# Three modulation weight units behind the experts, per-block waits at the layers' seams

## The chip, the cores and the metric

The kernel runs on one core of one Trainium2 chip. The metric is the device time of one execution in microseconds (us), less is better. Five engines run their own instruction streams and meet only at semaphores: PE (TensorE, matrix products into PSUM), DVE (VectorE), ACT (ScalarE), POOL (GpSimd) and SP (SyncE, which here issues nearly all DMAs, strictly in program order).

## The reference, cut to what matters

Three networks run one after the other on 256 tokens of width 1024, in fp32:

```
x = first_block(x, c, ...)    # Fourier + recurrent mixer, then a mixture of 16 experts
    h = modulate(rms_norm(x), sh2, sc2)
    gate, idx = top_k(softmax(h @ w_router), 32)          # each expert takes 32 of 256 tokens
    hid = silu(xs @ w_g[e]) * (xs @ w_u[e])               # 1024 -> 2816, e = 0..15
    x = x + gt2 * segment_sum((hid @ w_d[e]) * gate)      # 2816 -> 1024
x = second_block(x, c_2, ...) # attention and spatial gating, then relu^2 MLP
    x = x + gate1 * (merged @ w_out);  x = x + gate2 * (square(relu(h @ w_ff1)) @ w_ff2)
x = third_block(x, c_3, ...)  # two layers
    for l in (0, 1):
        shift, scale, gate = split(silu(c_3) @ w_ada_3[l] + b_ada_3[l], 3)     # 1024 x 3072
        proj = (rms_norm(x) * (1 + scale) + shift) @ w_in_3[l]
        x = x + gate * rms_norm(mix(proj) @ w_out_3[l])
```

The modulation of the third block's layer 0 (`w_ada_3[0]`) depends on `c_3` alone, so it may be computed at any time before that layer.

## The kernel before, in words

**Weights.** All weights stream once from HBM. A *unit* is one ring slot of 1.5 MB: 8 x 128 rows by 384 columns of a dense layer, or one 128-row piece of a modulation matrix (`w_ada`). `Plan` deals the units to four ring slots in the order of `CYCLE`; a unit's load is issued by SP once the unit before it in the slot is used (`unit_used`, counted by PE). During the expert stage the ring, the arena and `w_hi_raw` are twelve slots. An expert has 14 units (`EXPERT`); the first seven of expert 0 (`FIRST_CYCLE`) are loaded ahead, those of two slots in halves (`load_half`), and every later unit waits for PE to use the unit before it in its slot.

**Modulations.** `ada[p]` are eight units, each multiplied by `ada_unit` (16 matmuls into PSUM banks 6 and 7), copied out by ACT (`rows_out`), turned by PE (`turn`) and added to the bias by DVE (`mod_in`). `ada[4]`, the one for the third block's layer 0, is loaded and multiplied in the stage between the first block's mixer and expert 0.

**Dense layers.** A layer is cut into blocks of 128 output features, three to a unit. Each fp32 weight block is split in two parts: ACT copies the high part (`high_parts`, L1281, into one of four `w_hi` buffers), DVE subtracts for the low part (`low_parts`, L1684, counted as `w_split`). A block is then 24 matmuls: high x high, low x high, high x low, for eight chunks k of the input. The first three blocks of a layer run k-outer (`k_outer`, L769): for every chunk k the matmuls of all three blocks, so that they can start before the input is complete. The others run block by block (L818). Before its first matmul `k_outer` waits for the splits of all three blocks.

**Norms.** In the second and third block the RMS factor is applied behind the matmul ("raised"): ACT and DVE make the parts of a scaled X (`raise_x` L1309, `raise_low` L1813), squares are summed on DVE (L1793, L1805, L2101), PE adds over partitions (`column_sums` L849, L853), ACT takes the root, DVE the reciprocal (L1846), and only then can DVE empty the PSUM banks (`scale_rows` L1854). PE can run up to six blocks before that. `row_roots` lets DVE split the weight block `s0 + 4` between the sums' result and the reciprocal, where `s0` is the layer's first block; `s0 + 5` follows behind three `scale_rows`.

The seams are: experts to in2, proj2 to out2, out2 to ff1, ff2 to in3[0], in3[0] to out3[0], out3[0] to in3[1], in3[1] to out3[1].

## Time and profile before

| | us |
|---|---|
| median of 3 runs | 2250.39 (2247.58 to 2255.58) |
| the profiled execution, its own time | 2241.95 |
| its span in the trace | 2239.6 |
| PE busy | 1698.4 (76%) |
| DVE busy | 797.6 (36%) |
| ACT busy | 525.1 (23%) |
| mean granted TensorE clock, share of full speed | 0.857 |

The profiled execution took 2.35 us more than its span and 8.4 us less than the median of the runs. Busy shares are means over stages with different limits: the expert stage fills the middle of the span, and the dense layers stand on either side of it.

### The profile page before, as it was taken

What the parts mean: (1) busy time and instruction counts of PE and PEld (TensorE: products, weight loads), DVE (VectorE), ACT (ScalarE), POOL (GpSimd) and SP (SyncE); (2) the same over time, 40 slices, a digit from 0 to 9 for tenths busy, and PEclk for the clock granted to TensorE, in tenths of its full rate; (3) what the DMA queues carried; (4) which work ended last, traced back from release to release, by engine and by line L of the source; (5) the groups of instructions that cost most, each with busy time, mean ns of one, the idle gap of its engine ahead of it and who ended that gap; (6) DMA issues with size and microseconds to landing.
All of it is one profiled execution on the core that took longest, in us unless ns stands there. A gap on an engine that the chain in (4) does not pass through costs nothing.

```text
span 2239.6 us, 33790 instructions
## 1 busy us (share of the span) xinstructions
PE 1698.4 (76%) x14864; PEld 1168.7 (52%) x14864; DVE 797.6 (36%) x1237; ACT 525.1 (23%) x857; POOL 52.6 (2%) x85
## 2 busy tenths in 40 slices
PE   5999986656766666665665755665899999999897
PEld 4896843313322322322331322232798999998896
DVE  5766630000000000000000000010775788788777
ACT  2420220000000000000000000000574564365664
POOL 0014000000000000000000000000000000000000
PEclk8999997877777777777777787877999999999999
DMA  9877899999999999999999999999743559853541
GB/s 357 291 269 298 350 414 428 427 428 429 432 430 428 431 429 429 430 430 429 428 431 428 428 431 430 428 429 429 233 156 133 170 180 348 280 171 125 168 133 66
DMA packets 138723, 760.60 MB, mean 340 GB/s; under 512 B 7911, under 2 KB 96743, under 8 KB 106888
## 3 DMA queue, kind: packets, MB, share of 16 engines
q1 hardware_dynamic: 134968, 754.06, 83.7%
q10 hardware_dynamic: 3664, 5.24, 0.7%
q8 instruction: 68, 1.11, 0.2%
q14 instruction: 23, 0.19, 0.0%
HBM read 756.13 MB, written 3.14 MB: 339 GB/s over the span
## 4 chain that ended last, share of the span: by engine, by line
DMA 48%; PE 43%; DVE 6%; ACT 1%; issue 1%; SPq 1%; DVEq 0%; ACTq 0%
DMA ring<-in_w_exp_down 27%; PE ps L818 19%; DMA ring<-in_w_exp_up 18%; PE ps L1103 4%; PE ps L1233 4%; PE ps L1096 4%; DMA w_hi_raw<-in_w_exp_up 3%; PE ps L769 3%; DVE ring_lo L1684 1%; PE ps L692 1%; PE ps L1215 1%; PE ps L964 1%; PE ps L812 1%; PE ps L1148 1%; PE ps L874 0%
## 5 line engine op out<-in xcount | busy, mean ns | idle before, releaser
L1103 PE MATMUL ps<-arena,const 128*32 128x352 f32 x2816 | 340.6, 644 | 255.7 <-DMA arena<-in_w_exp_up 136.2
L1103 PEld LDWEIGHTS ps<-arena,const 128*32 128x32 f32 x2816 | 107.3, 143 | 476.0 <-DMA arena<-in_w_exp_up 170.9
L1684 DVE TENSOR_TENSOR ring_lo<-ring,w_hi 128x1024 fp32r<-128x1024 f32 x220 | 267.4, 1219 | 43.7 <-ACT w_hi L1281 42.7
L818 PE MATMUL ps<-u_hi,w_hi 128*128 128x258 f32 x960 | 275.5, 287 | 1.3 <-DVE ring_lo L1684 1.1
L2065 DVE TENSOR_TENSOR tail<-tail,ps 128x704 f32<-128x704 f32 x15 | 13.3, 888 | 734.4 <-PE ps L1103 734.4
L818 PE MATMUL ps<-u_hi,ring_lo 128*128 128x258 f32 x960 | 271.2, 282 | 0.0
L818 PE MATMUL ps<-u_lo,w_hi 128*128 128x258 f32 x960 | 271.0, 282 | 0.0
L1281 ACT ACTIVATE w_hi<-ring 128x1024 fp32r<-128x1024 f32 x220 | 230.2, 1050 | 69.0 <-PE ps L1233 30.5
L818 PEld LDWEIGHTS ps<-u_hi,w_hi 128*128 128x128 f32 x960 | 181.6, 189 | 7.3 <-issue 5.2
L1103 PE MATMUL ps<-ring,const 128*32 128x352 f32 x1024 | 126.0, 656 | 77.8 <-DMA ring<-in_w_exp_up 40.6
L818 PEld LDWEIGHTS ps<-u_lo,w_hi 128*128 128x128 f32 x960 | 181.6, 189 | 0.0
L818 PEld LDWEIGHTS ps<-u_hi,ring_lo 128*128 128x128 f32 x960 | 181.2, 189 | 0.0
L1096 PE MATMUL ps<-ring,const 128*32 128x256 f32 x1536 | 128.8, 503 | 58.1 <-DMA ring<-in_w_exp_down 58.1
L2069 DVE TENSOR_TENSOR arena<-arena,ps 128x2048 f32<-128x2048 f32 x15 | 34.3, 2288 | 373.1 <-PE ps L1119 373.1
L1096 PE MATMUL ps<-arena,const 128*32 128x256 f32 x896 | 86.6, 552 | 58.0 <-DMA arena<-in_w_exp_down 52.3
L1466 ACT ACTIVATE const<-ps 128x256 f32<-128x256 f32 x16 | 6.1, 383 | 525.6 <-PE ps L1055 525.6
L1103 PEld LDWEIGHTS ps<-ring,const 128*32 128x32 f32 x1024 | 39.8, 144 | 164.6 <-issue 58.2
L1096 PEld LDWEIGHTS ps<-ring,const 128*32 128x32 f32 x1536 | 59.4, 141 | 112.5 <-DMA ring<-in_w_exp_down 62.0
L1461 ACT ACT_TABLE_LOAD x15 | 19.2, 1283 | 397.1 <-PE ps L1103 397.1
L818 PE MATMUL ps<-x_parts,w_hi 128*128 128x256 f32 x592 | 107.7, 280 | 5.5 <-DVE ring_lo L1684 5.5
L1096 PEld LDWEIGHTS ps<-arena,const 128*32 128x32 f32 x896 | 43.0, 155 | 103.9 <-DVE const L2067 50.0
L818 PEld LDWEIGHTS ps<-x_parts,w_hi 128*128 128x128 f32 x592 | 91.5, 188 | 7.8 <-DVE ring_lo L1684 7.3
(287 smaller groups left out, 2357.9 us busy)
## 6 DMA issues: line engine op xcount, KB each, us to landing
arena<-in_w_exp_gate SPq DMA_DIRECT2D x45, 2816.0 KB, 35.5
ring<-in_w_exp_down SPq DMA_DIRECT2D x32, 3072.0 KB, 33.9
arena<-in_w_exp_up SPq DMA_DIRECT2D x32, 2816.0 KB, 36.1
ring<-in_w_in SPq DMA_DIRECT2D x37, 1536.0 KB, 7.0
arena<-in_w_exp_down SPq DMA_DIRECT2D x16, 3072.0 KB, 36.5
ring<-in_w_exp_gate SPq DMA_DIRECT2D x15, 2816.0 KB, 30.9
ring<-in_w_exp_up SPq DMA_DIRECT2D x15, 2816.0 KB, 31.7
ring<-in_w_ada SPq DMA_DIRECT2D x24, 1536.0 KB, 9.2
```

Of the source, the lines that this page charges most:

```text
L692: m = pe.matmul(ps[32 * j:32 * j + 32, 6 + i, 0:ADA_J // 2], conds[:, kc, :], slot(u, ADA_PASS)[:, at:at + ADA_J // 2], start=(kc == 0), s ...
L769: m = pe.matmul(ps[:, it["bank"], 0:a.shape[-1]], w, a, start=(n == 0 and j == 0), stop=(n == KD - 1 and j == 2), skip_group_check=True)
L812: m = pe.matmul(ps[:, bank, 2 * P * t:2 * P * t + 2 * P], a, w, start=(k == 0 and j == 0), stop=(k == KD - 1 and j == 2))
L818: m = pe.matmul(ps[:, bank, 0:a.shape[-1]], w, a, start=(k == 0 and j == 0), stop=(k == KD - 1 and j == 2))
L964: m = pe.matmul(o[:, :, half, :], KG[:, 4 * d + h, P * t:P * t + P], r[:, :, half, :], start=True, stop=True, skip_group_check=True)
L1096: m = pe.matmul(ps[32 * j:32 * j + 32, 4, 0:T], HIDT[:, k, :], SPACE[at][:, a:a + T], start=(k == 0), stop=(k == FC - 1), skip_group_check ...
L1103: m = pe.matmul(ps[32 * j:32 * j + 32, bank + h, 0:FJ // 2], XCUR[:, k, :], SPACE[at][:, a:a + FJ // 2], start=(k == 0), stop=(k == KD - 1 ...
L1148: m = pe.matmul(ps[:, 4 + i, T * t:T * t + T], QA[64 * i:64 * i + 64, c, P * t:P * t + P], KA[64 * i:64 * i + 64, c, :], start=True, stop= ...
L1233: m = pe.matmul(ps[:, it["b"] % 4, 0:T], w, a, start=(b == 0 and k == 0 and j == 0), stop=(b == FF // D - 1 and k == KD - 1 and j == 2), s ...
L1281: mark(act.activation(w_hi[:, s % HI, :, :], slot(c["u"], KD, c["w"])[:, :, c["col"]:c["col"] + P], ACT.Copy), "w_high")
L1684: tt(slot(c["u"], KD, c["w"], of=ring_lo)[:, :, at], slot(c["u"], KD, c["w"])[:, :, at], w_hi[:, s % HI, :, :].bitcast(F32), ALU.subtract) ...
L2069: tt(moe, moe, ps[:, 4:8, :], ALU.add).then_inc(S("acc_done"), 1)
```

## The change

It has four parts. (1) Three of the eight units of `ada[4]` leave the stage before the experts: unit 5 is loaded behind in2 and multiplied after in2, unit 6 after the spatial gating, unit 7 behind the first three blocks of out2. Their sum is a second pass (`LATE`) with its own `rows_out`, `turn` and `mod_in`, added to what the first pass left in `mod[:, 4]`. Unit 1 is multiplied inside out1. The halves of expert 0 are issued in another order and have semaphores of their own. (2) `k_outer` waits block by block, and its third block runs two chunks behind (`LAG`). (3) In in2 and in3[1] DVE's sums of squares stand behind the whole loop over chunks, the last adds are a tree of three, and PE's `column_sums` stands behind the fourth block of the layer (`SUMS_BEHIND`). (4) More weight blocks are split ahead of a seam (out1, out2, ff1).

```diff
+LATE = 5
+LAST = 6
+EARLY = 5
+LAG = (0, 0, 2)
+SUMS_BEHIND = 3
+TREE = 3
...
-    out1 = plan.dense(D, lambda n: ["cat"])
+    out1 = plan.dense(D, lambda n: ["cat"], after=lambda i: ada[4].append(plan.unit(at=spare)) if i == 0 else None)
-    ada[4] += [plan.unit(at=s) for s in (spare, o0, o1, o2, spare, o0, o1)]
+    ada[4] += [plan.unit(at=s) for s in (o0, o1, o2)[:EARLY - 2]]
...
+    ada[4] += [plan.unit() for _ in range(KD - EARLY - 1)]
...
-    out2 = plan.dense(D, lambda n: ["merged"])
+    out2 = plan.dense(D, lambda n: ["merged"], after=lambda i: ada[4].append(plan.unit()) if i == 0 else None)
...
             load_half(2, 0)
-            load_ada(4, range(2, 4))
+            load_ada(4, range(2, 3))
+            load_half(3, 0)
+            load_ada(4, range(3, 4))
             used(out1[-1]["u"])
+            load_ada(4, range(4, EARLY))
             load_expert(0, 5)
-            load_ada(4, range(4, KD))
+            load_half(3, 1)
+            load_half(4, 1)
             sp.wait_ge(S("h_turned"), 1)
             load_expert(0, 6)
             load_half(4, 0)
-            load_half(3, 0)
-            load_half(3, 1)
-            load_half(4, 1)
...
             def k_outer(g, lo, src, first, ready, each, order):
 
-                for it in g["items"]:
-                    pe.wait_ge(S("w_split"), it["s"] + 1)
-                    if it["b"] >= 4:
-                        pe.wait_ge(S("evacuated"), it["free"])
-                for n, k in enumerate(order):
-                    pe.wait_ge(S(ready), first + n + 1)
+                for step in range(KD + max(LAG)):
                     for i, it in enumerate(g["items"]):
+                        n = step - LAG[i]
+                        if not 0 <= n < KD:
+                            continue
+                        k = order[n]
+                        if n == 0:
+                            pe.wait_ge(S("w_split"), it["s"] + 1)
+                            if it["b"] >= 4:
+                                pe.wait_ge(S("evacuated"), it["free"])
+                        pe.wait_ge(S(ready), first + n + 1)
...
+                for i, _ in enumerate(dense_blocks(units, lambda it: (U_HI, U_LO), raise_input(), ready="u_split",
+                                                   each=each)):
+                    if i == behind:
+                        column_sums(two, TREE)
+                    yield
...
-            rest = raised_dense(in2, True)
+            rest = raised_dense(in2, True, SUMS_BEHIND)
...
             attention(rest, in2, QA2, KA2)
+            pe.wait_ge(S("pt_out"), ATT)
+            pe.wait_ge(S("ao_out"), PAIRS)
+            for kc in range(EARLY, KD - 2):
+                ada_unit(4, kc)
             pe.wait_ge(S("evacuated"), in2[-1]["items"][-1]["b"] + 1)
...
             count(m, "sgu")
+            ada_unit(4, KD - 2)
...
-            dense(out2)
+            dense(out2, after=lambda i: ada_unit(4, KD - 1) if i == 0 else None)
+            turn(LATE)
...
+            def sum_tree():
+
+                for n in (4, 2, 1):
+                    if n < 4:
+                        waits("sum1", made["sum1"])
+                    mark(tt(SQ[:, 0:n, :], SQ[:, 0:n, :], SQ[:, n:2 * n, :], ALU.add), "sum1")
...
-            low_parts(starts["in2"] + 2)
+            low_parts(starts["in2"] + 1)
             waits("scattered", EXPERTS + 1)
-            for i in range(KD + 2):
+            for i in range(KD + 1):
...
-                if i == 0:
-                    low_parts(starts["in2"] + 3)
-                if 1 <= i <= KD:
+                if i >= 1:
                     raise_low(S_IN2, i - 1)
-                if i >= 2:
-                    add_scaled_square(i - 2, GF2_IN2)
...
+                if i in (1, 2):
+                    low_parts(starts["in2"] + i + 1)
+            low_parts(starts["in2"] + HI)
+            for c in range(KD):
+                add_scaled_square(c, GF2_IN2)
+            sum_tree()
             row_roots(True, in2)
...
             group[0] = "end"
             low_parts(starts["out2"] + 3)
             raised_shift(mod[:, 3, 0:8])
+            low_parts(starts["out2"] + HI)
...
-                    low_parts(it["s"] + HI)
+                    low_parts(max(it["s"] + HI, starts["ff1"] + HI + 2))
...
+                if more:
+                    low_parts(in3[l + 1][0]["items"][0]["s"] + HI)
...
+                    sum_tree()
```

SP's queue between the mixer and expert 0, before: `w_ada` are units of `ada[4]`, loads of 128x2816 are halves or single units of expert 0, those of 128x5632 and 128x6144 its later units.

```order
L601 DMA arena<-in_w_exp_gate 128x2816 [waits x_split]
L520 DMA ring<-in_w_ada 128x3072 [waits unit_used] x2
L520 DMA w_hi_raw<-in_w_exp_up 128x2816 [waits unit_used]
L520 DMA ring<-in_w_ada 128x3072 [waits unit_used] x4
L520 DMA arena<-in_w_exp_up 128x2816 [waits h_turned]
L601 DMA ring<-in_w_exp_up 128x2816 [waits unit_used]
L601 DMA ring<-in_w_exp_gate 128x2816 [waits unit_used] x2
L601 DMA ring<-in_w_exp_up 128x2816 [waits unit_used]
L520 DMA arena<-in_w_exp_up 128x5632 [waits unit_used] x2
```

The same place in the changed kernel:

```order
L608 DMA arena<-in_w_exp_gate 128x2816 [waits x_split]
L527 DMA ring<-in_w_ada 128x3072 [waits unit_used]
L608 DMA ring<-in_w_exp_gate 128x2816 [waits unit_used]
L527 DMA ring<-in_w_ada 128x3072 [waits unit_used] x2
L527 DMA w_hi_raw<-in_w_exp_up 128x2816
L608 DMA ring<-in_w_exp_gate 128x2816 [waits unit_used]
L608 DMA ring<-in_w_exp_up 128x2816 [waits unit_used]
L527 DMA arena<-in_w_exp_up 128x2816 [waits h_turned]
L608 DMA ring<-in_w_exp_up 128x2816 [waits unit_used]
L527 DMA arena<-in_w_exp_up 128x5632 [waits unit_used] x2
```

Three `w_ada` loads are gone, and three of the four ring halves of expert 0 stand ahead of the wait for `h_turned`, one of them inside out1.

DVE at the seam from the experts to in2, before, from the last chunk on: L1813 is the low part of X, L1793 the scaled sum of squares, L2101 the plain sum, L1684 the split of a weight block, L1846 the reciprocal.

```order
L1813 SCALAR_TENSOR_TENSOR u_lo<-X,cols,u_hi 128x256 [waits u_high]
L1793 SCALAR_TENSOR_TENSOR rs<-arena,cols,rs 128x256 [waits sum2,x_squared] x2
L2101 TENSOR_TENSOR arena<-arena 128x256
L2101 TENSOR_TENSOR arena<-arena 128x256 [waits sum1] x6
L1684 TENSOR_TENSOR ring_lo<-ring,w_hi 128x8x128 [waits w_high]
L1839 TENSOR_SCALAR rs<-ps 128x256 [waits summed]
L1840 SCALAR_TENSOR_TENSOR rs<-rs,ps 128x256 [waits dve_step]
L1684 TENSOR_TENSOR ring_lo<-ring,w_hi 128x8x128 [waits w_high,mean_square]
L1846 RECIPROCAL rs<-rs 128x256 [waits rooted]
```

The same place in the changed kernel (L1852, L1822 and L1825, L1844, L1715 and L1885 are the same operations):

```order
L1852 SCALAR_TENSOR_TENSOR u_lo<-X,cols,u_hi 128x256 [waits u_high] x2
L1715 TENSOR_TENSOR ring_lo<-ring,w_hi 128x8x128 [waits w_high]
L1822 TENSOR_SCALAR rs<-arena,cols 128x256 [waits x_squared]
L1825 SCALAR_TENSOR_TENSOR rs<-arena,cols,rs 128x256 [waits sum2,x_squared] x7
L1844 TENSOR_TENSOR arena<-arena 128x1024
L1844 TENSOR_TENSOR arena<-arena 128x512 [waits sum1]
L1844 TENSOR_TENSOR arena<-arena 128x256 [waits sum1]
L1878 TENSOR_SCALAR rs<-ps 128x256 [waits summed]
L1879 SCALAR_TENSOR_TENSOR rs<-rs,ps 128x256 [waits dve_step]
L1715 TENSOR_TENSOR ring_lo<-ring,w_hi 128x8x128 [waits w_high,mean_square]
L1885 RECIPROCAL rs<-rs 128x256 [waits rooted]
```

The split of the layer's fourth weight block stands ahead of the sums now, and all eight scaled squares, which were spread over the loop, stand behind it.

## Rows read from the trace of the kernel before

**Rows 1.** The page's chain that ended last, shares by engine.

```profile
DMA 48%; PE 43%; DVE 6%; ACT 1%; issue 1%; SPq 1%; DVEq 0%; ACTq 0%
```

**Rows 2.** Busy time by stretch: PE, PEld, DVE, ACT, POOL, clock, DMA share, GB/s.

```profile
260.00:285.00 25.00, 22.44 (x189) 21.70 (x190) 17.00 (x34) 8.31 (x13) 0.00 (x0) 1.00 0.71 260
285.00:320.00 35.00, 32.04 (x313) 18.72 (x316) 15.91 (x38) 9.81 (x21) 1.27 (x4) 0.90 1.01 428
320.00:1570.00 1250.00, 791.33 (x7508) 336.01 (x7500) 83.44 (x70) 48.98 (x77) 15.27 (x44) 0.77 1.00 429
...
1581.00:1584.00 3.00, 3.00 (x15) 3.00 (x15) 3.00 (x9) 2.40 (x7) 0.00 (x0) 0.50 1.06 373
```

**Rows 3.** Timeline of SP's queue, 267 to 320: start, us, what.

```profile
283.25 6.18 SPq L520 DMA_DIRECT2D ring<-in_w_ada  x4
...
313.38 4.26 SPq L520 DMA_DIRECT2D arena<-in_w_exp_up  x2
```

**Rows 4.** The DMAs issued at about 277.5 and at 313.38: KB, us to landing.

```profile
ring<-in_w_ada SPq DMA_DIRECT2D x1, 1536.0 KB, 6.5
...
arena<-in_w_exp_up SPq DMA_DIRECT2D x1, 2816.0 KB, 15.1
```

**Rows 5.** Timeline of PE before expert 0: start, us, what.

```profile
304.12 3.87 PE L1046 MATMUL ps<-arena 128*128 128x32 f32 x32 [0.38 <-DVE arena L2053]
307.93 2.79 PE L692 MATMUL ps<-ring,conds 128*32 128x384 f32 x16
310.49 2.82 PE L1103 MATMUL ps<-arena,const 128*32 128x352 f32 x32
```

**Rows 6.** Timeline of PE, ACT and DVE at the seam to in2.

```profile
1580.74 0.49 PE L769 MATMUL ps<-u_hi,w_hi 128*128 128x258 f32 x1 [3.48 <-DVE u_lo L1813]
...
1587.88 1.07 DVE L1793 SCALAR_TENSOR_TENSOR rs<-arena,cols,rs 128x256 f32<-128x256 f32 x2
1588.86 3.18 DVE L2101 TENSOR_TENSOR arena<-arena 128x256 f32<-128x256 f32 x7
1591.96 1.22 DVE L1684 TENSOR_TENSOR ring_lo<-ring,w_hi 128x1024 fp32r<-128x1024 f32 x1
...
1595.33 1.75 DVE L1846 RECIPROCAL rs<-rs 128x256 f32<-128x256 f32 x1
...
1598.11 1.22 DVE L1684 TENSOR_TENSOR ring_lo<-ring,w_hi 128x1024 fp32r<-128x1024 f32 x1
...
1588.94 1.06 ACT L1281 ACTIVATE w_hi<-ring 128x1024 fp32r<-128x1024 f32 x1
```

**Rows 7.** The chain that ended last, pieces at the other seams: start, us, what.

```profile
1599.39 14.66 PE ps L818 x120
...
1707.80 1.24 DVE arena L2187
...
1746.61 14.41 PE ps L818 x120
...
1763.03 8.20 PE ps L769 x66
...
1940.78 1.24 PE ps L748 x12
...
1948.30 1.14 DVE ring_lo L1684
...
1949.79 8.18 PE ps L769 x66
...
2070.25 13.89 PE ps L818 x120
...
2085.07 0.71 PE ps L849 x2
...
2090.88 10.52 PE ps L769 x66
...
2102.55 20.15 PE ps L818 x168
```

More of the change, by code:

```diff
@@ L686, in ada_unit @@
                 unit_ready(u)
-                if kc == 0 and p > 0:
-                    pe.wait_ge(S("rows_out"), p)
+                first, last = (0, KD - 1) if p != 4 else (0, EARLY - 1) if kc < EARLY else (EARLY, KD - 1)
+                if kc == first and p > 0:
+                    pe.wait_ge(S("rows_out"), p if kc < EARLY else LATE)
                 for i in range(2):
@@ L692, in ada_unit @@
                         m = pe.matmul(ps[32 * j:32 * j + 32, 6 + i, 0:ADA_J // 2], conds[:, kc, :],
-                                      slot(u, ADA_PASS)[:, at:at + ADA_J // 2], start=(kc == 0),
-                                      stop=(kc == KD - 1), skip_group_check=True)
+                                      slot(u, ADA_PASS)[:, at:at + ADA_J // 2], start=(kc == first),
+                                      stop=(kc == last), skip_group_check=True)
                 count(m, "unit_used")
@@ L823, in dense_blocks, with dense @@
                         yield
-            def dense(units, order=range(KD)):
-                for _ in dense_blocks(units, lambda it: (X_HI, X_LO), split_input(), order=order):
+            def dense(units, order=range(KD), after=lambda i: None):
+                for _ in dense_blocks(units, lambda it: (X_HI, X_LO), split_input(), after, order=order):
                     pass
@@ L843, in _, with column_sums @@
             sums = [0, 0]
-            def column_sums(two):
-                sums[0] += KD - 1
+            def column_sums(two, adds=KD - 1):
+                sums[0] += adds
                 pe.wait_ge(S("sum1"), sums[0])
@@ L855, in column_sums, with raised_dense @@
                 count(m, "summed")
-            def raised_dense(units, two):
+            def raised_dense(units, two, behind=None):
                 def each(k, i):
-                    if k == KD - 1 and i == (2 if units is in2 else 0):
+                    if behind is None and k == KD - 1 and i == 0:
                         column_sums(two)
-                return dense_blocks(units, lambda it: (U_HI, U_LO), raise_input(), ready="u_split", each=each)
+                for i, _ in enumerate(dense_blocks(units, lambda it: (U_HI, U_LO), raise_input(), ready="u_split",
[3 more added lines that the diff above has]
+                    yield
             norms = [0]
@@ L1013, in _ @@
             count(m, "o_spread")
-            dense(out1)
+            dense(out1, after=lambda i: ada_unit(4, 1) if i == 0 else None)
             column_sums(False)
-            for kc in range(1, 4):
+            for kc in range(2, EARLY - 1):
                 ada_unit(4, kc)
@@ L1033, in _ @@
             count(m, "aff_turned")
-            for kc in range(4, 6):
-                ada_unit(4, kc)
+            ada_unit(4, EARLY - 1)
             pe.wait_ge(S("pos"), 1)
@@ L1080, in landed @@
                 def landed(i):
+                    if not later and i < FIRST_CYCLE and EXPERT[i][3] not in SINGLE_AT:
+                        pe.wait_ge(S(f"half{i}"), 32)
+                        return
                     pe.wait_ge(w_ready[EXPERT[i][3]], e * (16 * 2) + plan.ready[exp0 + EXP_UNITS * later + i] - later * 16 * 2)
@@ L1432, in _ @@
             group[0] = "in2"
-            high_parts(starts["out1"] + 3)
+            high_parts(starts["out1"] + HI)
             act.preload_act_table(ACT.Sqrt)
@@ L1488, in _ @@
             result(EXPERTS - 1)
-            high_parts(starts["in2"] + 3)
+            high_parts(starts["in2"] + 2)
             for c in range(KD):
                 raise_x(S_IN2, c, "x_new", c + 1)
+                if c == 0:
+                    high_parts(starts["in2"] + 3)
             act.preload_act_table(ACT.Sqrt)
@@ L1581, in _ @@
                     evacuate(it, (SQ, XN)[it["src"]][:, it["n"], :])
-                high_parts(starts["out2"] + min(2 * i + 1, 3))
+                high_parts(starts["out2"] + min(2 * i + 1, HI))
             act.preload_act_table(ACT.Sqrt)
@@ L2023, in _ @@
                 split(CAT, HEADS + h)
+            low_parts(starts["out1"] + HI)
             residual(out1, mod[:, 0, 16:24])
@@ L2091, in _ @@
                              X[:, i, :], ALU.mult, ALU.add), "x_new")
-                if i == 0:
-                    low_parts(starts["in2"] + 3)
-                if 1 <= i <= KD:
+                if i >= 1:
                     raise_low(S_IN2, i - 1)
-                if i >= 2:
-                    add_scaled_square(i - 2, GF2_IN2)
-            for c in range(1, KD):
-                if c > 1:
-                    waits("sum1", made["sum1"])
-                mark(tt(SQ[:, 0, :], SQ[:, 0, :], SQ[:, c, :], ALU.add), "sum1")
+                if i in (1, 2):
[4 more added lines that the diff above has]
+            sum_tree()
             row_roots(True, in2)
```

57 lines of the change are left out of this document (33 added, 24 removed).

## The prediction

> **What bounds the kernel now.** I read the chain that ended last first. The reader is to see that it is nearly all DMA (48%) and PE (43%) [rows 1]. The stretches say where which holds. From 320 to 1570, the experts, the DMA engines are busy all the time at 429 GB/s while PE is busy 791 of 1250 us: DMA bounds [rows 2]. Behind the experts the chain is PE, in pieces of 8 to 20 us with short waits at the seams [rows 7]. So bytes taken out of the expert stage count as long as the queue stays full, and behind it every matmul and every wait of PE counts. The third view is the stretch ahead of the experts: from 260 to 285 the DMA engines are busy only 0.71, from 285 on 1.01 [rows 2]. There SP issues four modulation units from 283.25 to 289.4, then the loads of expert 0, and the first load that needs a slot freed by expert 0 at 313.38 [rows 3]. It lands 15.1 us later, at 328.5 [rows 4].
>
> **Three units out of the stage.** They are 3 x 1.573 MB, at 429 GB/s 11.0 us. One half of expert 0 (1.44 MB, 3.4 us) also moves into the slack between 260 and 285. If the queue stayed full, the stage would end 14.4 us earlier. It doesn't stay full: all twelve slots are then loaded early, and the next load waits until PE has used the first unit of expert 0. From 283 on the changed queue holds one modulation unit and five loads of 1.44 MB, 8.8 MB or 20.5 us, and is empty at about 306. PE's side: the gather of expert 0's tokens ends at 304.12 + 3.87 = 308.0; behind it stood one more modulation unit (2.79 us, overlapped in part), and the first unit of expert 0, 32 matmuls in 2.82 us, began at 310.49 [rows 5]. Without that unit it begins when ACT has copied the tokens, some 0.4 us behind 308.0, ends at 311.3, and SP issues at 311.4. What a load takes in an empty queue I take from the one at 277.5: 6.5 us for 1.573 MB, of which 3.7 us are data, so 2.8 us are fixed [rows 4]. For 2.884 MB that makes 2.8 + 6.7 = 9.5, so it lands at 320.9 instead of 328.5. From there both queues hold the same bytes. Term: **-7.6**. Bounds: -2.0 (only the earlier issue, if the 15.1 us were not a queue) and -11.0 (the bytes alone).
>
> For the same load the Trainium skill, "DMA: Bandwidth & Descriptors", section "Anatomy of one DMA", has another fixed part: about 2.0 us and the bytes at 436 GB/s (fitted there for GpSimd's queue). By it the load would take 8.6 us, land at 320.0, and the term would be -8.5.
>
> **The three units behind the experts.** Each is 16 matmuls, 1.4 us at full clock (2.79 at half [rows 5]); the turn is 1.24 [rows 7]; together 5.4 us of PE. They stand where PE waits anyway: before the spatial gating (about 1.1 us for the last evacuation), behind it (DVE's 1.24 us add at 1707.80, which PE must await), and behind the first three blocks of out2 (1.10 us before 1746.61, for a weight split that is now made earlier) [rows 7]. Each overhangs its cover by 0.1 to 0.3. Term: **+0.6**; without cover +4.2 for the units, the turn being counted below. Their loads join a stage whose DMA engines are half idle. In SP's queue the loads of proj2 stand behind units 5 and 6, whose slots are free some 20 us before proj2 needs its weights.
>
> **out2 to ff1.** Before, the last block of out2 ends at 1746.61 + 14.41 = 1761.0, and `k_outer` starts at 1763.03, because the split of its third weight block comes behind the last update [rows 7]. Now two blocks start at once behind the turn, at 1762.3, and the third has its split when its turn comes. The sums stand in step 7 and come out 1.6 us earlier, the split of the sixth block stands behind the first `scale_rows`, and the 1.1 us wait there (its piece is not in the rows) goes. 2.0 - 1.24 + 1.1 and rounding: **-2.1**; between -0.5 and -3.1 (all waits gone, turn too).
>
> **ff2 to in3[0].** The same wait: split from 1948.30 for 1.14, start at 1949.79, block end 1947.8 [rows 7]. Nothing fills it now. **-1.9**, and no second wait to win. Bounds 0 and -2.0.
>
> **in3 to out3, twice.** Here PE isn't late for a weight split but for chunks: DVE makes them one by one while `k_outer` runs, up to 2.1 us before 2070.25. After the last awaited chunk (the seventh) `k_outer` had 18 matmuls to do; with the third block two chunks behind it has 24. Six more at 0.12 us (14.41 / 120 [rows 7]) are 0.7, the first time less 0.17 of slack at 2070.25: **+1.3** for both. Bounds 0 and +1.5.
>
> **Experts to in2.** This is the place to look at. Before, PE starts at 1580.74, DVE ends its sums at 1588.86 + 3.18 = 1592.0, and the layer's sixth block starts at 1599.39 [rows 6, 7]. Between the two lies a chain that the change leaves alone: PE's sums (1.2), two small operations and a weight split on DVE (2.1), the reciprocal (1.75), three `scale_rows` (1.0), a split (1.22): 7.35 us. What counts is when the sums are done. Changed: chunks come 1.1 us earlier, since two splits no longer stand ahead of X, and at 0.8 instead of 1.2 us each. But then DVE waits for ACT's copy of the fourth weight block. That copy stands behind ACT's eight chunks and a table load; before it began at 1588.94 [rows 6], now at about 1587.7. It ends at 1588.8, the split at 1590.0. Only then come the eight scaled squares: 0.53 each (1.07 for two [rows 6]), 4.2 in all, so 1594.2. The tree adds 1024, 512 and 256 columns: 1.2 (as the split of 1024 [rows 6]), 0.7 between, and 0.45 (3.18 / 7), 2.4 in all. Sums done at 1596.6, sixth block at 1603.9: **+4.5**. PE starts `k_outer` 1.7 us earlier and does four blocks by 1593.4, then waits 3 us for the sums and 2 us for the fifth block's split, which was covered by the fourth block before. Bounds: -1.7 (only the earlier start) and +6.
>
> **out3[0] to in3[1].** The start is 0.1 us earlier, `k_outer` still bound by PE. Before, behind it from 2102.55 seven blocks run without a gap [rows 7]. Changed, it ends at about 2101.8; the fourth block, then the sums, until 2105.3. Only then can DVE scale and split the fifth block's weights (1.8): 2107.0. Reciprocal, scales and split (4.0) end at 2111.0, where the sixth block stood at 2102.55 + 5.76 = 2108.3. **+2.7**. Bounds -0.6 (the sums' own place in the k-outer part) and +3.5.
>
> In1 and out1 gain and lose a few tenths by the lag and the unit in out1: 0, within 0.7 either way.
>
> **Sum.** -7.6 + 0.6 - 2.1 - 1.9 + 1.3 + 4.5 + 2.7 = -2.5. The profiled execution took 2241.95, so 2239.4 beside it; the runs' median was 2250.39, so **2247.9**. What this measurement can tell from no change is about 0.3%, 6.8 us.
>
> **Rivals.** (A) The forecast: gain at the experts, given back at two seams. Chance 0.50, own range 2244 to 2252.
> (B) The seams pay too: ACT's copy or the squares come sooner than I reckon, and the sums are covered. Then the two big terms are 0 and -0.2: 2247.9 - 7.4 = 2240.5. For it speaks that DVE's sums lose four operations, against it that DVE has 0 us of idle time before 1592 to win and now waits for ACT. 0.27.
> (C) Slower: the clock. With PE idle from 2085.8 to 2090.88, the first 24 matmuls of `k_outer` ran at about half rate (10.52 us for 66 instead of 7.9 [rows 7]); behind the wait of 3.48 us the granted clock was 0.50 from 1581 to 1584 [rows 6, 2], that is 1.2 of 2.4 GHz. If the new waits of 3 and 2 us in in2 and 1.8 and 1.1 us in in3[1] bring the same drop, each costs up to 2.6: 2247.9 + 5.2 = 2253.1, and slower than before from the second drop on. 0.13.
> (D) The load at 311.4 finds no advantage beyond its earlier issue (-2.0): 2253.5. Rows 4 speak against it: 15.1 us for 6.7 us of data is a queue. 0.06.
> (E) The units cost their full PE time: +3.6, 2251.5. 0.04.
>
> The page "TensorE: Matmul & The Clock Gate" of the Trainium skill ("What's actually happening") says that the throttled clock is the default and only activity releases it. By this rule C is the expected course at every new wait, and the time is C's 2253.1; waits of 2.0 us at 1763 and 1949 left the pieces behind them at full rate [rows 7], and so I keep it at 0.13.
>
> From these: faster by over 0.3% (below 2243.6) 0.25, nearly all of B; slower by over 0.3% (above 2257.1) 0.06, of C and D; the rest the same. The range takes in B's time and C's and D's: 2240 to 2254.
>
> **What would show it.** The first load behind expert 0's first unit should land near 321 and the DMA share dip between 306 and 313. In in2 the sums on DVE should end some 19 us behind the last expert's scatter, and PE wait 3 us behind the fourth block. PE should start ff1 and in3[0] without a gap. The forecast is wrong if the experts end less than 5 or more than 10 us earlier, or if no wait stands behind the fourth block of in2.

## The result and the profile after

The changed kernel takes 2256.49 us (median of 20 runs, 2250.72 to 2261.40) against 2250.47 us of the kernel before (20 runs): ratio 1.0032, 95% interval 1.0021 to 1.0042, so it is slower by 7.2 us (4.7 to 9.5). The forecast was 2247.9, with a range of 2240 to 2254. The profiled execution took 2253.26 us, its span is 2251.0.

The chain that ended last has the same shape as in [rows 1]:

```profile
DMA 49%; PE 43%; DVE 5%; ACT 1%; issue 1%; SPq 1%; DVEq 0%; ACTq 0%
```

**Ahead of the experts.** Timeline of SP's queue (start, us, what), then the DMA issued last there with its time to landing; they answer to [rows 3, 4]:

```profile
300.69 0.33 SPq L527 DMA_DIRECT2D arena<-in_w_exp_up  x1
303.52 0.33 SPq L608 DMA_DIRECT2D ring<-in_w_exp_up  x1
320.96 4.26 SPq L527 DMA_DIRECT2D arena<-in_w_exp_up  x2
...
arena<-in_w_exp_up SPq DMA_DIRECT2D x1, 2816.0 KB, 9.1
```

The queue runs empty near 309 (I reckoned 306), and the load then takes 9.1 us (I reckoned 9.5). But it is issued at 320.96 and not at 311.4, so it lands at 330.1 and not at 320.9. The stretches show it (columns as in [rows 2]): from 310 to 322 the DMA engines are busy 0.09, and TensorE's granted clock is 0.58, between its two levels of 1.2 and 2.4 GHz.

```profile
285.00:310.00 25.00, 16.86 (x107) 12.22 (x107) 15.21 (x40) 10.20 (x20) 0.60 (x3) 0.72 0.89 351
310.00:322.00 12.00, 11.53 (x73) 8.57 (x72) 1.48 (x1) 1.09 (x2) 0.67 (x2) 0.58 0.09 23
322.00:1570.00 1248.00, 790.35 (x7571) 335.27 (x7575) 82.83 (x66) 48.98 (x77) 15.27 (x44) 0.77 1.01 429
```

PE's timeline in this stretch, first before, then after (L1023 and L1043 are the router's matmuls, L1028 and L1048 transposes of the tokens, L692 and L703 modulation units, L1064 the gather for which before's row stands in [rows 5], L1123 the first unit of expert 0):

```profile
289.08 4.05 PE L1023 MATMUL ps<-WR,arena 128*128 128x16 f32 x32
292.98 2.73 PE L1028 MATMUL ps<-const,arena 128*128 128x128 f32 x16
...
296.06 3.42 PE L692 MATMUL ps<-ring,conds 128*32 128x384 f32 x32
```

```profile
291.25 5.92 PE L1043 MATMUL ps<-WR,arena 128*128 128x16 f32 x32 [1.33 <-ACT arena L1374]
297.01 3.65 PE L1048 MATMUL ps<-const,arena 128*128 128x128 f32 x16
...
301.02 2.43 PE L703 MATMUL ps<-ring,conds 128*32 128x384 f32 x16
306.97 0.39 PE L1057 MATMUL ps<-const 16*128 16x16 f32 x2 [3.52 <-DVE const L2089]
309.17 7.04 PE L1064 MATMUL ps<-arena 128*128 128x32 f32 x32 [1.81 <-DVE arena L2093]
316.68 4.20 PE L1123 MATMUL ps<-arena,const 128*32 128x352 f32 x32 [0.47 <-ACT const L1483]
```

The same work takes longer: router 5.92 instead of 4.05 us, transposes 3.65 instead of 2.73, gather 7.04 instead of 3.87. I had carried the durations of before over. But of the six units that stood ahead of the gather three are gone: unit 1, which is inside out1 now, and units 5 and 6 (unit 7 stood behind it). Over the gather and the first matmuls behind it the granted clock (the number before the DMA share) is 0.81 before and 0.54 after. The third line is that of before_thin, an experiment below that has before's loads but hardly multiplies four units:

```profile
305.00:314.00 9.00, 9.00 (x81) 5.33 (x80) 1.43 (x1) 1.19 (x2) 0.62 (x2) 0.81 1.01 422
309.00:321.00 12.00, 11.36 (x66) 8.40 (x66) 1.88 (x2) 1.09 (x2) 1.27 (x4) 0.54 0.03 12
308.00:322.00 14.00, 13.65 (x76) 10.56 (x76) 2.06 (x2) 1.20 (x2) 1.28 (x4) 0.56 1.00 410
```

**Seams behind the experts.** Pieces of the chain that ended last (they answer to [rows 7]):

```profile
1602.43 19.07 PE ps L834 x144
...
1770.19 7.31 PE ps L785 x60
...
1954.59 10.93 DMA arena<-bias_rows
1965.52 3.16 issue
1970.96 16.18 PE ps L834 x120
...
2078.19 14.15 PE ps L834 x120
...
2098.97 10.22 PE ps L785 x72
2109.19 2.89 PE ps L834 x24
...
2114.29 19.05 PE ps L834 x144
```

ff1 and in3[0] start without a wait. But behind in3[0]'s fifth block the chain now runs through a DMA, `arena<-bias_rows`. In2's seam on DVE (answers to [rows 6]; L1715 weight split, L1822 and L1825 scaled squares, L1844 the tree):

```profile
1588.40 0.48 DVE L1852 SCALAR_TENSOR_TENSOR u_lo<-X,cols,u_hi 128x256 fp32r<-128x256 f32 x1 [0.19 <-ACT u_hi L1336]
1591.08 1.22 DVE L1715 TENSOR_TENSOR ring_lo<-ring,w_hi 128x1024 fp32r<-128x1024 f32 x1 [2.19 <-ACT w_hi L1308]
1592.22 0.35 DVE L1822 TENSOR_SCALAR rs<-arena,cols 128x256 f32<-128x256 f32 x1
1592.67 4.02 DVE L1825 SCALAR_TENSOR_TENSOR rs<-arena,cols,rs 128x256 f32<-128x256 f32 x7
1596.61 2.40 DVE L1844 TENSOR_TENSOR arena<-arena 128x1024 f32<-128x1024 f32 x3
```

### The profile page after: what moved, and what is told of

Its sections match the earlier page's. It is cut to its first block, busy times and chain, and to the rows that moved or that the text cites. A ratio compares the mean times of both kernels' runs of the same rounds, so it can differ in the third digit from the quotient of the medians.

```text
span 2251.0 us, 33795 instructions
## 1 busy us (share of the span) xinstructions
PE 1709.0 (76%) x14876; PEld 1179.7 (52%) x14876; DVE 798.6 (35%) x1230; ACT 525.3 (23%) x858; POOL 52.3 (2%) x85
## 4 chain that ended last, share of the span: by engine, by line
DMA 49%; PE 43%; DVE 5%; ACT 1%; issue 1%; SPq 1%; DVEq 0%; ACTq 0%
DMA ring<-in_w_exp_down 27%; PE ps L834 19%; DMA ring<-in_w_exp_up 19%; PE ps L1123 4%; PE ps L1259 4%; PE ps L1116 3%; PE ps L785 3%; DMA w_hi_raw<-in_w_exp_up 2%; PE ps L703 1%; PE ps L984 1%; PE ps L1240 1%; DVE ring_lo L1715 1%; PE ps L828 1%; PE ps L1168 1%; DMA arena<-bias_rows 0%
## 5 line engine op out<-in xcount | busy, mean ns | idle before, releaser
L1123 PE MATMUL ps<-arena,const 128*32 128x352 f32 x2816 | 337.9, 640 | 251.8 <-DMA arena<-in_w_exp_up 131.2
L1123 PEld LDWEIGHTS ps<-arena,const 128*32 128x32 f32 x2816 | 106.2, 142 | 471.8 <-DMA arena<-in_w_exp_up 164.7
L1715 DVE TENSOR_TENSOR ring_lo<-ring,w_hi 128x1024 fp32r<-128x1024 f32 x220 | 267.3, 1218 | 53.3 <-ACT w_hi L1308 52.1
L2105 DVE TENSOR_TENSOR tail<-tail,ps 128x704 f32<-128x704 f32 x15 | 13.3, 888 | 728.5 <-PE ps L1123 728.5
L1123 PE MATMUL ps<-ring,const 128*32 128x352 f32 x1024 | 127.6, 663 | 81.8 <-DMA ring<-in_w_exp_up 42.1
L1123 PEld LDWEIGHTS ps<-ring,const 128*32 128x32 f32 x1024 | 40.0, 145 | 168.1 <-issue 59.8
```

The source lines that it names most:

```text
L1123: m = pe.matmul(ps[32 * j:32 * j + 32, bank + h, 0:FJ // 2], XCUR[:, k, :], SPACE[at][:, a:a + FJ // 2], start=(k == 0), stop=(k == KD - 1 ...
L1715: tt(slot(c["u"], KD, c["w"], of=ring_lo)[:, :, at], slot(c["u"], KD, c["w"])[:, :, at], w_hi[:, s % HI, :, :].bitcast(F32), ALU.subtract) ...
```

## The experiments

**One table for all.** Single runs scatter by 10 us and more, so I read every kernel's timeline at the same five events, and only differences within a stretch. *Issue*: from the router's first matmul to the end of expert 0's first 32 matmuls, which lets SP issue the first freed load. *Landing*: from that end to the last piece of weights of the experts (start of the last 48 matmuls that waited for a DMA). *Stage*: both together. *Seams*: from the end of the last expert's scatter to PE's last matmul. For the kernel before: 313.31 - 289.08 = 24.2; 1570.87 - 313.31 = 1257.6; 2228.84 - 1577.27 = 651.6. The ratio is taken over all runs of the kernel and of before on the same chip; it differs from the quotient of the two medians by up to 0.0017. The other columns are read from one profile each.

| kernel | ratio to before (95%) | gather | issue | landing | stage | seams |
|---|---|---|---|---|---|---|
| before | 1 | 3.87 | 24.2 | 1257.6 | 1281.8 | 651.6 |
| before_again | 1 | 4.00 | 24.9 | 1256.9 | 1281.8 | 652.5 |
| changed | 1.0032 (1.0021, 1.0042) | 7.04 | 29.6 | 1253.1 | 1282.8 | 660.6 |
| units_only | 1.0004 (0.9991, 1.0018) | 7.03 | 29.6 | 1253.0 | 1282.6 | 653.6 |
| seams_only | 1.0015 (1.0001, 1.0030) | 3.76 | 25.8 | 1256.0 | 1281.8 | 660.5 |
| before_thin | 1.0015 (0.9997, 1.0034) | 7.03 | 29.9 | 1253.2 | 1283.1 | 655.4 |
| warm | 1.0009 (0.9995, 1.0024) | 3.76 | 23.2 | 1253.1 | 1276.3 | 656.5 |
| warm_gather | 1.0009 (0.9989, 1.0029) | 5.55 | 25.2 | 1252.9 | 1278.0 | 657.9 |
| bias_late | 1.0012 (0.9997, 1.0026) | 7.03 | 29.3 | 1252.9 | 1282.3 | 656.9 |
| in2_old | 1.0014 (0.9993, 1.0035) | 7.04 | 29.6 | 1253.2 | 1282.8 | 655.0 |
| in31_old | 1.0018 (0.9993, 1.0044) | 7.03 | 29.6 | 1253.2 | 1282.8 | 659.4 |
| lag0 | 1.0035 (1.0020, 1.0050) | 7.03 | 29.3 | 1253.1 | 1282.4 | 657.0 |
| best1 | 0.9963 (0.9944, 0.9983) | 7.04 | 27.9 | 1252.9 | 1280.9 | 649.7 |
| best2 | 0.9981 (0.9961, 1.0002) | 3.83 | 23.2 | 1252.8 | 1276.0 | 651.1 |
| best3 | 0.9979 (0.9963, 0.9994) | 7.04 | 29.8 | 1252.9 | 1282.7 | 648.8 |
| best4 | 0.9980 (0.9960, 0.9999) | 7.04 | 28.4 | 1253.1 | 1281.5 | 649.2 |
| best5 | 0.9981 (0.9964, 0.9997) | 10.19 | 30.3 | 1252.9 | 1283.2 | 648.7 |

(Gather in best5 and warm_gather with the dummy work inside it.)

**units_only, seams_only.** The change split in its two halves, each put alone into the kernel before:

```diff
 # units_only: before, and of the change only this
+LATE, LAST, EARLY = 5, 6, 5        # units 5, 6, 7 behind in2, behind the gating, in out2
 # seams_only: before, and of the change only this
+LAG, SUMS_BEHIND, TREE = (0, 0, 2), 3, 3   # k_outer, in2, in3[1], splits ahead
```

> The kernel before with only the three units moved behind the experts (and the halves of expert 0 in the changed order, unit 1 inside out1). Theory 1 (the routing stretch loses its filling work, TensorE's granted clock falls there, and expert 0's first unit is used 7.6 us later, so that nothing is gained): within 2 us of before or slower, 2250 to 2254, and the first load freed by expert 0 issued at about 320. Rival (my forecast: issue at 311.4, landing at 321): 2243.5.

> The kernel before with the seams changed (waits per block, third block two chunks behind, sums behind the chunks, splits ahead) and all eight units of ada[4] left in the stage before expert 0. Theory 1 (read from the profile after: the seams cost +5.8 at in2, -1.9 at ff1, +1.6 at in3[0], +1.1 at out3, +2.5 at in3[1]): slower than before by 6 to 9 us, 2256 to 2259. Rival (the units are what costs, the seams are near my forecast of +2.5): 2253.

units_only: no gain, issue 29.6. This is theory 1. The seams alone cost 8.9 us in their stretch against the profile of before and 8.0 against before_again; by the ratio the kernel is 3.4 us slower (0.2 to 6.8), less than theory 1's 6 to 9. The median of 2252.99 is the rival's 2253.

**before_again.** The kernel before, unedited.

> The kernel before once more, for a second profile: the first was taken from an execution 8 us below the median. If the stretches that the change leaves alone (up to out1, the experts) carry that difference, they are longer here and the seams behind the experts stay as they were to 0.5 us (in2's first block to the spatial gating 125.0, in3[0] to in3[1] 141.1). If the seams themselves vary from run to run, these two differ by more.

Its span is 5.5 us longer, of which 4.4 stand ahead of the router (293.44 against 289.08). The stage is equal to 0.1 us, and in2 to the gating takes 125.04 us in both. In3[0]'s first block to in3[1]'s is 143.1 instead of 141.1, more than the 0.5 us I expected, and the seams as a whole are 0.9 longer. Of the 2.0 us, 1.5 are in3[0]'s first block: behind the same wait of 2.02 us it takes 4.65 us here (granted clock 0.62) and 3.12 in the profile of before (1.00).

**before_thin.** The loads of before, four units of the routing stretch hardly multiplied:

```diff
+                        if p == 4 and kc in (3, 5, 6, 7) and (i, j) != (1, CG - 1):
+                            continue
```

> The kernel before, its loads and slots unchanged, but four of the eight units of ada[4] (3, 5, 6 and 7, those of the routing stretch) are multiplied with one of their eight matmuls only; so the layer-0 modulation lacks that part of its sum. Theory 1 (the matmuls of the units hold TensorE's granted clock up): without them router and gather take 5 to 6 and 7.04 us as in the changed kernel, the first freed load is issued some 29 us behind the router's first matmul instead of 24, and the kernel is 2 to 6 us slower than before although it computes less. Rival (the clock falls in the changed kernel because of the changed loads or their order): 4.06 and 3.87 us as before, 24 us or less, and not slower.

PE's timeline:

```profile
291.17 5.56 PE L1025 MATMUL ps<-WR,arena 128*128 128x16 f32 x32 [0.68 <-ACT arena L1349]
296.57 3.58 PE L1030 MATMUL ps<-const,arena 128*128 128x128 f32 x16
...
308.35 7.03 PE L1048 MATMUL ps<-arena 128*128 128x32 f32 x32 [0.64 <-DVE arena L2055]
```

With all loads in their old place and only matmuls taken away, the router takes 5.56 us and the gather 7.03 (5.92 and 7.04 in the changed kernel), and the issue comes at 29.9. So the missing matmuls, not the changed loads, are the cause. That the kernel does less work and gains nothing also shows in the ratio (1.0015, not told from 1).

**warm, warm_gather.** Dummy matmuls in the changed kernel where the units stood, the size of one unit each (`keep_warm`, three times; in warm_gather two half groups inside the gather too):

```diff
+            def keep_warm():
+                for _ in range(2):
+                    for j in range(CG):
+                        pe.matmul(ps[32 * j:32 * j + 32, 4, 0:ADA_J // 2], conds[:, 0, :],
+                                  X[:, 0:2, :].rearrange("p a b -> p (a b)")[:, 0:ADA_J // 2], ...)
...
             for kc in range(2, EARLY - 1):
                 ada_unit(4, kc)
+            keep_warm()
...
             ada_unit(4, EARLY - 1)
+            keep_warm()
             pe.wait_ge(S("pos"), 1)
...
+            keep_warm()
             pe.wait_ge(S("sel"), 1)
```

> The changed kernel with three dummy groups of matmuls (the size of a modulation unit each, into an unused PSUM bank, result not read) in the routing stretch where the three units stood. Theory 1: the granted clock stays at 1.0 through the router's matmuls and the gather (4.06, 2.73 and 3.87 us again instead of 5.92, 3.65 and 7.04), the first freed load is issued at 313 to 315 instead of 321, and the kernel is 5 to 7 us faster than the changed one: 2250. Rival (the lateness comes from work and loads placed ahead, not from the clock): more work on TensorE, issue at 321 or later, 2256 to 2260.

> The changed kernel with the dummy groups of warm and two half groups (0.75 us each at full clock) inside the gather. Theory 1 (the gather, 32 matmuls of 32 columns, is too thin to bring the clock back once it has fallen, so that it runs at half rate to its end in some executions): with wide matmuls in between it takes 5.3 us at full clock, 6.5 at most, never 8.5. Rival (the clock falls for a fixed time, whatever the matmuls in the gather are): 8.5 us (7.04 and 1.5), and 0 to 3 us slower than warm.

PE's timeline in warm:

```profile
288.21 4.06 PE L1052 MATMUL ps<-WR,arena 128*128 128x16 f32 x32
292.12 2.67 PE L1057 MATMUL ps<-const,arena 128*128 128x128 f32 x16
...
301.32 1.50 PE L712 MATMUL ps<-X,conds 128*32 128x384 f32 x16
303.20 3.76 PE L1075 MATMUL ps<-arena 128*128 128x32 f32 x32 [0.38 <-DVE arena L2104]
307.44 3.93 PE L1134 MATMUL ps<-arena,const 128*32 128x352 f32 x32 [0.47 <-ACT const L1494]
```

Three more groups of wide matmuls, and the first unit of expert 0 is done 6.4 us earlier (23.2 instead of 29.6). The whole stage is 6.5 us shorter in this profile, as theory 1 had it, and the ratio falls from 1.0032 to 1.0009. But the profiled execution (2239.83 us) was the fastest of warm's twelve, whose median is 2251.74, so the profile may show more than the usual gain. warm_gather: the gather took 5.55, within theory 1. But see best5.

**bias_late.** DVE's wait for the attention bias at its first use:

```diff
                 row_roots(l == 0, in3[l])
-                waits("bias_in", 32)
...
+                def bias_of(h):
+                    if l == 0 and h == 0:
+                        waits("bias_in", 32)
+                    return BIAS[:, h, :]
-                softmax(in3[l], lambda h: BIAS[:, h, :],
+                softmax(in3[l], bias_of,
```

> The changed kernel with DVE's wait for the attention bias (a DMA of 1 MB twice, issued by ACT behind ff2, landing some 14 us later) moved from ahead of the scale_rows of in3[0] to the first use of the bias in the softmax. Theory 1: the 3.2 us that DVE idled before its scale_rows and PE's 2.1 us wait behind in3[0]'s fifth block go, with the lower clock behind it: 3 to 4 us faster than the changed kernel, 2253. Rival (DVE waited there for something else, or the wait reappears at the softmax): no change.

DVE at in3[0] (L1885 reciprocal, L1893 `scale_rows`), first the changed kernel, then bias_late:

```profile
1963.77 1.74 DVE L1885 RECIPROCAL rs<-rs 128x256 f32<-128x256 f32 x1
1968.68 1.09 DVE L1893 TENSOR_TENSOR tail<-ps,rs 128x258 f32<-128x258 f32 x3 [3.17 <-issue]
```

```profile
1966.96 1.74 DVE L1885 RECIPROCAL rs<-rs 128x256 f32<-128x256 f32 x1
1968.74 1.09 DVE L1893 TENSOR_TENSOR tail<-ps,rs 128x258 f32<-128x258 f32 x3
```

The idle time is gone, the seams are 3.7 us shorter, the ratio goes from 1.0032 to 1.0012. Theory 1 holds. "issue" in a profile can be a wait for a DMA. For the kernel before, the tile's view gives the two issues and their landings:

```profile
L1606 ACTq DMA_DIRECT2D arena<-bias_rows x2: 395/498/600, 1948.3 to 1948.8; - x2
...
DMA to landing us min/median/max: 11.0/12.2/13.3
```

1948.8 + 13.3 = 1962.1, and before's `scale_rows` began at 1962.7: the DMA had 0.6 us to spare there (2.2 in before_again, where PE comes later: 1968.2 against 1952.7 + 13.3).

**in2_old, in31_old.** One seam each as before (squares in the loop, `column_sums` at its old place):

```diff
 # in2_old
-            rest = raised_dense(in2, True, SUMS_BEHIND)
+            rest = raised_dense(in2, True)      # and DVE's and ACT's code of before there
 # in31_old
-                attention(raised_dense(in3[l], l == 0, SUMS_BEHIND if l > 0 else None), ...)
+                attention(raised_dense(in3[l], l == 0, None), ...)   # and DVE's loop of before
```

> The changed kernel with the seam from the experts to in2 alone as it was: scaled squares in the loop, seven adds, TensorE's column_sums behind the third block, the weight splits in the old places (waits per block and the lagging third block stay). Theory 1 (the late sums and the half clock that follows the thinner feeding cost 7 us there): the stretch from in2's first block to the spatial gating is 125 to 126 us instead of 132.1, and the kernel 5 to 7 us faster than the changed one, 2250. Rival (per-block waits and the lagging third block alone cause it): 131 to 132, no gain.

> The changed kernel with the seam from out3[0] to in3[1] alone as it was (squares and adds in the loop over chunks, column_sums inside the first blocks). Theory 1: the changed place costs 2.5 to 2.9 us there, so in3[1]'s first block to out3[1]'s is 110 to 110.5 instead of 112.6, and the kernel 2 to 3 us faster than the changed one. Rival (the lagging third block is what costs): under 1 us.

in2_old: in2's first block to the gating 125.3 instead of 132.1; since PE starts 1.7 us later again, 5.1 of it count (scatter to gating 128.7 instead of 133.9). Seams 655.0, ratio 1.0014, which is 4 us less than the changed kernel where I expected 5 to 7. DVE there:

```profile
1594.70 0.47 DVE L1850 SCALAR_TENSOR_TENSOR u_lo<-X,cols,u_hi 128x256 fp32r<-128x256 f32 x1
1595.09 1.06 DVE L1823 SCALAR_TENSOR_TENSOR rs<-arena,cols,rs 128x256 f32<-128x256 f32 x2
1596.08 3.18 DVE L2137 TENSOR_TENSOR arena<-arena 128x256 f32<-128x256 f32 x7
1599.17 1.22 DVE L1713 TENSOR_TENSOR ring_lo<-ring,w_hi 128x1024 fp32r<-128x1024 f32 x1
```

The weight split stands behind the sums, which end 14.8 us behind the scatter (1599.3 - 1584.5), against 19.4 in the changed kernel (1599.0 - 1579.6). in31_old: in3[1] to out3[1] 110.3 instead of 112.6 as expected, but the stretch behind is 0.8 longer, and the seams as a whole are 1.2 shorter. Neither ratio is told from the changed kernel's by its interval.

**lag0.** `LAG = (0, 0, 0)` in the changed kernel.

> The changed kernel with the third block of k_outer no longer two chunks behind. Theory 1 (my term of +1.3 for the two out3 layers, of which the profile shows 1.2): the stretch from in3[0] to in3[1] and that behind in3[1] 0.5 to 0.7 us shorter each; ff1 and in3[0], where the third block then needs its weight split at once, lose up to 2 us each again; in all -1 to +3 us against the changed kernel. Rival (the lag costs nothing): +3 to +4.

The stretches behave as in theory 1: 0.8 us less from out3[0] to in3[1] and 0.8 less behind out3[1]'s start, 0.7 more from ff1 to in3[0]. In3[0] to out3[0] is also 2.3 shorter, since in3[0] starts later and the bias is waited for less. The ratio doesn't move (1.0035), which is inside theory 1's -1 to +3 us, though the profile's seams are 3.6 us shorter.

**best1, best2, best3, best4, best5.** The changed kernel mended:

```diff
 # best1 = warm + bias_late + in2_old + in31_old;  best2 = best1 with LAG = (0, 0, 0)
 # best3 = best1 with keep_warm(times=2) behind unit 4, from a constant tile
 # best4 = best3 and
+            keep_warm(bank=3, times=2)
             rest = raised_dense(in2, True)
...
                 column_sums(False)
+                if l == 0:
+                    keep_warm(bank=6, times=3)
 # best5 = best1 with the half groups of warm_gather
```

> The changed kernel with four things together: the dummy matmuls in the routing stretch, the wait for the bias at its first use, and the seams to in2 and to in3[1] as before. Theory 1 (terms -6.5, -3.9, -6 and -2.5 against the changed kernel): 2237 to 2240, that is 10 us faster than before. Rival (the terms read from single profiles overstate what the medians move by): 2243 to 2247.

> best1 with the third block of k_outer no longer two chunks behind. Theory 1: as for the changed kernel, -1 to +3 us against best1. Rival: +3 to +4.

> The kernel with four changes (best1) and more dummy work in the routing stretch: two groups instead of one behind the transposed affinities, where TensorE still idled 2.5 to 3.0 us; the groups read a constant tile now. Theory 1 (TensorE's idle time of 3 us ahead of the gather is what lets the granted clock fall): the gather takes 3.8 to 3.9 us instead of 7.04, the first freed load is issued 3 to 5 us earlier than in best1 counted from the router's first matmul, and the median is 2 to 4 us below best1's. Rival (the gather's slow clock has another cause): 7.04 again, no change.

> best3 with dummy matmuls in two more waits: two groups (3.0 us) between the last expert's scatter and in2, three groups (4.5 us) between out3[0]'s sums and in3[1]. Theory 1 (the first blocks behind those waits run at half clock because TensorE idled): the k-outer part of in2 takes 9 to 10 us instead of 10.4 and that of in3[1] 8.9 to 9.5 instead of 10.2 to 10.5, 1 to 3 us less in all. Rival (these parts are bound by the chunks from VectorE, whatever the clock): the same durations, no gain, or a loss where the dummy work overhangs the wait.

> best1 with the two half groups of dummy matmuls inside the gather, as in warm_gather. Theory 1 (they bring the clock back inside the gather in every execution, where best1 did so in some): the gather takes 5.3 to 5.6 us, the first unit of expert 0 ends some 25 us behind the router's first matmul instead of 27.9, and the median is 0 to 3 us below best1's, 2238 to 2241. Rival (best1 is at this already, and the 1.5 us of dummy work in the chain are lost): 2242 to 2244.

best1 measured 2241.09, against 2248.49 for before on the same chip: 0.37% faster, and 0.69% (0.9963 / 1.0032) faster than the changed kernel. That lies between theory 1 and its rival. In its profile nearly all of that stands in the seams (649.7 against 660.6); the gather is at 7.04 us and the stage 1.9 us shorter. best2 (0.9981) lies within best1's interval: the lag makes no difference that shows. All five mended kernels lie between 0.9963 and 0.9981. best3 refutes what I expected of it: more dummy work, only 1.9 us of idle time ahead, and the gather at 7.04 all the same. best5 (2246.06, where I expected 2238 to 2241 and the rival said 2242 to 2244) refutes the story of warm_gather, here PE's timeline (L1080 gather, L1076 and L712 dummy work):

```profile
308.70 0.39 PE L1067 MATMUL ps<-const 16*128 16x16 f32 x2 [3.16 <-DVE const L2103]
309.02 2.79 PE L712 MATMUL ps<-X,conds 128*32 128x384 f32 x16
311.74 1.92 PE L1080 MATMUL ps<-arena 128*128 128x32 f32 x8
313.59 1.51 PE L1076 MATMUL ps<-X,conds 128*32 128x384 f32 x8
315.03 1.92 PE L1080 MATMUL ps<-arena 128*128 128x32 f32 x8
316.88 1.51 PE L1076 MATMUL ps<-X,conds 128*32 128x384 f32 x8
318.31 3.62 PE L1080 MATMUL ps<-arena 128*128 128x32 f32 x16
```

Wide matmuls run at half rate here (1.51 instead of 0.85) and don't bring the clock back before the gather is over. best4: k-outer of in2 in 9.65 instead of 10.41 us, but PE then waits 1.71 instead of 0.94 for DVE's sums, and scatter to gating is 128.7 in both; that of in3[1] takes 11.1 us instead of 11.2 in best3. The rival is right, and in in2 the part is bound by DVE.

## Why the prediction was wrong, step by step

**Three units out of the stage: forecast -7.6, measured +1.0.** This step failed, and in it the time at which the first freed load is issued: the sentence "Without that unit it begins when ACT has copied the tokens, some 0.4 us behind 308.0, ends at 311.3". The shape was right: the queue is empty, the load takes 9.1 us, and from there the stage runs on a fixed course. The column *landing* shows it best: 1252.8 to 1253.2 in all thirteen kernels without the units' loads, and in before_thin, whose issue is as late. Where all units are loaded and the issue is early enough (24.2 in before, 24.9 in before_again, 25.8 in seams_only), the stage is 1281.8 all three times, set by bytes: the issue could come up to 1281.8 - 1253.0 = 28.8 us behind the router without a loss. The change takes bytes out and makes the issue the bound, and the same change moves the issue from 24.2 to 29.6. I had forecast 22.3 (311.4 - 289.1), which with 1253.0 gives 1275.3, a gain of 6.5. The 7.3 us between the two are the slower clock: router +1.9 us, transposes +0.9, gather +3.2, first unit of expert 0 +1.4 (4.20 instead of 2.82) in the rows above, 7.4 together. I counted the three units as load and as PE work, not as what kept TensorE busy between thin matmuls of 16 to 128 columns and DVE's top-k. Rival C named the clock, but only at the seams. By the rule of the Trainium skill, "TensorE: Matmul & The Clock Gate" ("What's actually happening"), that only activity releases the throttled clock, which I had weighed there, a slower clock was to be expected in this stretch as well; the trace agrees in direction (0.58 from 310 to 322). A smaller slip changed nothing: 20.5 us of loads from 283 on end at 303.5 and not at 306, and the queue ran empty near 309.

**Units behind the experts: +0.6, measured +0.6.** Ahead of the gating 4.74 instead of 4.50 us between the last attention block and proj2 (1716.85 - 1712.11; 1709.17 - 1704.67), behind out2's first blocks 1.43 instead of 1.10.

**out2 to ff1: -2.1, measured -2.2.** From the end of out2's k-outer part to ff2 it is 1863.12 - 1753.20 = 109.9 us instead of 111.8, and 0.3 of the 109.9 belong to the unit.

**ff2 to in3[0]: -1.9, measured +1.6 against the profile of before and +0.1 against three others.** The second step that failed. "Nothing fills it now" is right, in3[0] starts at once. But from the end of ff2 to the end of in3[0]'s tenth block it is 33.5 instead of 31.9 us (1987.07 - 1953.59; 1979.66 - 1947.77). Starting 2.0 us earlier meant reaching the wait for the bias before its DMA had landed; ACT issues it 0.6 us behind ff2's last matmul in both kernels, and it took 14.0 us here. The new wait is 2.1 us for PE, and the block behind it ran slow (120 matmuls in 16.18 instead of 14.3 us). I wrote "no second wait to win" and did not ask for one to lose. The 31.9 us are not the rule either: the same code takes 33.4 us in before_again, before_thin and units_only, because the first block behind the old wait of 2.02 us takes 4.6 us there instead of 3.1. Against these the change swaps one wait and its slow block for another and gains nothing. My reading in the rivals, that waits of 2.0 us leave the piece behind them at full rate, held at in3[0] in one profile of four; at ff1 it held in before and before_again and failed in before_thin.

**in3 to out3, twice: +1.3, measured +1.2** (12.65 us from in3's last block to the end of k-outer, twice; before 12.12 and 11.94).

**Experts to in2: +4.5, measured +5.2.** Scatter's end to the sixth block 27.3 us (1606.9 - 1579.6), before 22.1. DVE's links came as reckoned: it waits for ACT's copy (2.19 us), and its sums end 19.4 us behind the scatter. PE's came later than I wrote: it ends the fourth block at 1597.5 and not at 1593.4, so that it waits 1.5 us for the sums instead of 3, and 2.2 for the split; the sums come last either way. The last 0.7 are the fifth block at a lower clock, 4.5 us instead of 2.9 after two waits, so a piece of rival C.

**out3[0] to in3[1]: +2.7, measured +2.3** (k-outer's start to the sixth block 19.7 instead of 17.4).

The sum is 1.0 + 0.6 - 2.2 + 1.6 + 1.2 + 5.2 + 2.3 = 9.7 us against the profile of before; the medians moved by 6.0, and the ratio says 7.2 (4.7 to 9.5). In seams_only the profile also shows more than the ratio (8.9 against 3.4). A part of this lies in the profile of before, an execution 8 us below the median. Its seams, 651.6 us, are the shortest of the four profiles that have the old seams: 652.5 in before_again, 653.6 in units_only (with the units in them), 655.4 in before_thin. The difference is mostly the clock behind the old waits of 2.0 us: at ff1 the first block takes 4.55 us in before_thin and 3.12 in before, at in3[0] see above. Against before_thin seams_only loses 5.1 us and not 8.9. How often either course is taken in the executions that were not profiled isn't shown.

The mended parts add up in the ratios: against 1.0032, warm -0.0023, bias_late -0.0020, in2_old -0.0018, in31_old -0.0014 make -0.0075, and best1 has -0.0069. This is weak support for the single parts. Their own intervals are 0.0015 (warm, bias_late), 0.0021 and 0.0026 wide to either side, and the changed kernel's is 0.0011; the first two parts are barely told from nothing, the last two aren't, and only best1's gain over the changed kernel is well clear.

**Open:** why dummy matmuls help only at times. With the real units the gather ran at full clock in 3 of 3 profiles (3.76 to 4.00), without anything in their place in 0 of 7, with dummy work in 3 of 7 wholly or for the most part (warm, best2, warm_gather), though warm and best1 hold the same instructions in this stretch. The profiles of warm and best2 are the fastest of their twelve runs each (2239.83 and 2234.31 us; medians 2251.74 and 2242.06), so the full clock may be the rarer course there. No run tells what decides it.

## What to carry to other kernels

Work that fills an engine's waits may be what keeps its clock up: before you move such filler away, price the thin matmuls around it at both clock levels (here 3.87 and 7.04 us for one gather) and ask which transfer is released by the last of them. Taking bytes out of a DMA-bound stage gains only down to the point where the issue of the next load bounds it; work out that point first (here 4.6 us of slack in the issue, which the change used up). When a seam is tightened, list every wait of the engines in it, the hidden ones too, with its cover in us: the one that had 0.6 us to spare took back the whole 2.0 us that the seam had gained. And take a second profile of the kernel before, before a seam is priced: here its seams came out at 651.6 to 655.4 us with the same code.

## What was not expected of the hardware

The same 32 matmuls of the gather took 3.76 to 4.00 or 7.03 to 7.04 us, and no value in between where nothing stood inside it, even in two kernels with the same instructions around it (warm and best1). A load of 2.9 MB into an empty queue took 9.1 us, against 15.1 in a full one [rows 4]. And before_thin, with 4.7 MB more to load in the stage than the changed kernel, ends it only 0.3 us later (1283.1 against 1282.8), since the issue bounds both.
